# Two-block transformer kernel: 512-column pairing of the two activation halves in the residual and up stages, with a reduce and an in-place product on VectorE

## The reference, cut to what matters

```python
x = x + mixed @ w_out[l]                      # layers 0 and 1: 1024 x 1024
h = rms_norm(x, norm_ffn[l])
up = h @ w_up[l]                              # 1024 x 5632
a, bval = up[..., :D_FF], up[..., D_FF:]      # D_FF = 2816
a = conv(a, conv_w, width 3) + conv_b
x = x + (silu(a) * bval) @ w_down[l]          # 2816 x 1024
...
x = x + mix @ w_out                           # layer 2 (the second block)
m = rmsnorm(x, norm_mlp_w)
u = relu(m @ w_ff1)                           # 1024 x 4096
x = x + (u * u) @ w_ff2                       # 4096 x 1024
```

## Time and profile before

| | us |
|---|---|
| median of three runs | 1192.5 |
| lowest and highest run | 1192.38, 1197.29 |
| span of the profiled execution, first to last instruction | 1191.5 |
| TensorE busy (matmuls) | 1145.0 |
| VectorE busy | 725.3 |
| ScalarE busy | 586.5 |
| GpSimd busy | 358.4 |
| mean granted TensorE clock, share of full | 0.981 |

### The profile page before, as it was taken

The page is one execution under the profiler, slowest core; times in us unless marked ns, Lnnn a source line. Parts: engine busy times, 40 slices in busy tenths (PEclk is TensorE's granted clock), DMA queues, the critical chain, the costliest instruction groups (busy, mean ns, idle before and its releaser), DMA issues.

```text
span 1191.5 us, 21228 instructions
## 1 busy us (share of the span) xinstructions
PE 1145.0 (96%) x9016; PEld 1107.0 (93%) x9016; DVE 725.3 (61%) x1077; ACT 586.5 (49%) x800; POOL 358.4 (30%) x215
## 2 busy tenths in 40 slices
PE   6999999999999999999899999999889989999997
PEld 5998989999999999899899999998789989999996
DVE  5742227777576665222777766767778657756663
ACT  5444337555354635443755544566554646443432
POOL 3025644322022212645432302323443125101021
PEclk8999999999999999999999999998889989999999
DMA  8634334454754664343355475454322135573741
GB/s 282 204 106 142 107 116 150 160 177 137 252 178 130 194 209 141 106 135 114 110 174 177 157 232 178 147 166 146 93 71 72 54 124 184 162 219 123 238 133 58
DMA packets 172766, 180.43 MB, mean 151 GB/s; under 512 B 4224, under 2 KB 170496, under 8 KB 172544
## 3 DMA queue, kind: packets, MB, share of 16 engines
q1 hardware_dynamic: 172672, 179.08, 46.6%
HBM read 178.02 MB, written 1.05 MB: 150 GB/s over the span
## 4 chain that ended last, share of the span: by engine, by line
PE 72%; issue 11%; DVE 9%; ACT 5%; POOL 2%; DMA 1%; SPq 0%; POOLq 0%; DVEq 0%; ACTq 0%
PE psum L569 71%; ACT sb_w_hi L1064 2%; DVE sb_scratch L1498 2%; DVE sb_w_lo L1507 1%; POOL sb_scratch L2200 1%; PE psum L726 1%; DVE sb_rs L1546 1%; DVE sb_rs L1498 1%; ACT sb_scratch L1064 1%; DMA sb_raw<-in_w_in 1%; ACT sb_rs L1064 1%; DVE sb_xt L1498 0%; DVE sb_scratch L1927 0%; PE psum L800 0%; DVE sb_scratch L1747 0%
## 5 line engine op out<-in xcount | busy, mean ns | idle before, releaser
L569 PE MATMUL psum<-sb_xg_hi,sb_w_hi 128*128 128x256 f32 x1664 | 485.3, 292 | 4.5 <-DVE sb_w_lo L1507 3.1
L569 PE MATMUL psum<-sb_xg_lo,sb_w_hi 128*128 128x256 f32 x1664 | 474.6, 285 | 0.0
L569 PE MATMUL psum<-sb_xg_hi,sb_w_lo 128*128 128x256 f32 x1664 | 474.2, 285 | 0.0
L1507 DVE TENSOR_TENSOR sb_w_lo<-sb_raw,sb_w_hi 128x2048 fp32r<-128x2048 f32 (+3 forms) x147 | 301.2, 2052 | 129.1 <-ACT sb_w_hi L1064 129.1
L1064 ACT ACTIVATE sb_w_hi<-sb_raw 128x2048 fp32r<-128x2048 f32 (+3 forms) x189 | 319.6, 1698 | 118.2 <-PE psum L569 65.2
L569 PEld LDWEIGHTS psum<-sb_xg_hi,sb_w_hi 128*128 128x128 f32 x1664 | 323.1, 194 | 14.6 <-issue 10.3
L569 PEld LDWEIGHTS psum<-sb_xg_lo,sb_w_hi 128*128 128x128 f32 x1664 | 323.3, 194 | 0.7
L569 PEld LDWEIGHTS psum<-sb_xg_hi,sb_w_lo 128*128 128x128 f32 x1664 | 323.0, 194 | 0.0
L569 PE MATMUL psum<-sb_hid_hi,sb_w_hi 128*128 128x256 f32 x864 | 247.5, 286 | 8.8 <-DVE sb_hid_lo L1572 8.0
L2155 POOL TENSOR_TENSOR sb_w_lo<-sb_raw,sb_w_hi 128x2048 fp32r<-128x2048 f32 (+1 forms) x42 | 188.1, 4478 | 212.6 <-ACT sb_w_hi L1064 212.6
L569 PE MATMUL psum<-sb_hid_lo,sb_w_hi 128*128 128x256 f32 x864 | 245.5, 284 | 0.0
(11 more groups left out here) (144 smaller groups left out, 1006.1 us busy)
## 6 DMA issues: line engine op xcount, KB each, us to landing
sb_raw<-in_w_in SPq DMA_DIRECT2D x52, 1024.0 KB, 5.1
sb_raw<-in_w_up SPq DMA_DIRECT2D x44, 1024.0 KB, 5.1
sb_raw<-in_w_ff SPq DMA_DIRECT2D x16, 1024.0 KB, 5.5
sb_raw<-in_w_down SPq DMA_DIRECT2D x16, 768.0 KB, 4.4
sb_raw<-in_w_down SPq DMA_DIRECT2D x16, 640.0 KB, 4.1
sb_raw<-in_w_ff SPq DMA_DIRECT2D x16, 640.0 KB, 4.0
sb_raw<-in_w_out SPq DMA_DIRECT2D x8, 1024.0 KB, 5.0
sb_raw<-in_w_ff SPq DMA_DIRECT2D x8, 768.0 KB, 4.4
```

The costliest lines, as they stand in the source:

```text
L569: return nc.tensor.matmul(ps, lhsT, rhs, start=start, stop=stop, skip_group_check=True)
L1507: v.tensor_tensor(part(w_lo, s), part(raw, s), part(w_hi, s).bitcast(F32), ALU.subtract)\
```

## The change

For tiles of the kinds x, fa, fb and f2 a chunk's first two matmuls, which have the same weights (`hi`), become one of 512 columns: its moving operand is the chunk's high and low activation side by side, for which `xg_hi`/`xg_lo` and `hid_hi`/`hid_lo` become halves of one buffer. The left half of the bank gathers high by high and low by high, the right half high by low. Such a tile fills a bank of its own, and `Plan.place` deals the banks out; other kinds still share a bank in twos. The reader sums the halves. An x tile is added in two steps, left half and then right half, with a wait of VectorE for itself between them. In fa, fb and f2 tiles `tensor_reduce` sums both halves of the bank into SBUF in one pass, VectorE waits for that, and the product of before follows in place, reading SBUF only. The bank's reader is now the reduce (`a_sum`, `h_sum`, `r_sum`). `paired` gives the last tile of a bank, so a wide tile's reader waits for that tile alone.

```diff
@@ READERS, class Plan @@
+               "pb": ["yb_gated"], "x": ["x_tile"], "fa": ["a_sum"], "fb": ["h_sum"], "conv": ["c_tile"],
+               "ba": ["ba_tile"], "lg": ["lg_tile"], "z": ["z_tile"], "f2": ["r_sum"]}
+    WIDE = ("x", "fa", "fb", "f2")
+    def place(self):
+        self.banks, self.at = [], []
+        for t, kind in enumerate(self.kinds):
+            if kind in self.WIDE or t % 2 == 0:
+                self.banks.append([])
+            self.at.append((len(self.banks) - 1, len(self.banks[-1])))
+            self.banks[-1].append(t)
@@ build @@
-        xg_hi = sb("xg_hi", KD * T, F32R)
-        xg_lo = sb("xg_lo", KD * T, F32R)
+        xg_both = sb("xg_both", 2 * KD * T, F32R)
+        xg_hi, xg_lo = xg_both[:, 0:KD * T], xg_both[:, KD * T:]
...
         def main_bank(t):
-            return psum[:, t // 2 % RING, t % 2 * T:(t % 2 + 1) * T]
+            n, half = plan.at[t]
+            return psum[:, n % RING, half * T:(half + 1) * T]
+        def wide_bank(t):
+            return psum[:, plan.at[t][0] % RING, :].rearrange("p (two c) -> p two c", two=2)
         def paired(t):
-            return t // 2 * 2 + 2
+            return plan.banks[plan.at[t][0]][-1] + 1
@@ main_tile @@
-                if first and t % 2 == 0 and t >= 2 * RING:
-                    for name, value in plan.readers[t - 2 * RING] + plan.readers[t - 2 * RING + 1]:
-                        if q.due(name, value):
-                            pe.wait_ge(S[name], value)
+                bank, half = plan.at[t]
+                if first and half == 0 and bank >= RING:
+                    for before in plan.banks[bank - RING]:
+                        for name, value in plan.readers[before]:
+                            if q.due(name, value):
+                                pe.wait_ge(S[name], value)
...
+                    ends = last and k == s.chunks - 1
+                    if plan.kinds[t] in plan.WIDE:
+                        i = act[3] + k0 + k
+                        pair = split_pair(act[4])[:, :, i * T:(i + 1) * T]
+                        mul(wide_bank(t), hi[:, k, c], pair, first and k == 0, False)
+                        mm = mul(main_bank(t), lo[:, k, c], pair[:, 0, :], False, ends)
+                        continue
@@ x_add @@
-                v.tensor_tensor(tl(xt, m), tl(xt, m), main_bank(t), ALU.add).then_inc(S["x_tile"], 1)
+                parts = wide_bank(t)
+                v.tensor_tensor(tl(xt, m), tl(xt, m), parts[:, 0, :], ALU.add).then_inc(S["dve_step"], q.one("dve_step"))
+                dve.wait_ge(S["dve_step"], q.sent["dve_step"])
+                v.tensor_tensor(tl(xt, m), tl(xt, m), parts[:, 1, :], ALU.add).then_inc(S["x_tile"], 1)
+            def sum_wide(out_, t, signal):
+                v.tensor_reduce(out_, wide_bank(t).rearrange("p two c -> p c two"), mybir.AxisListType.X, ALU.add)\
+                    .then_inc(S[signal], q.one(signal))
+                dve.wait_ge(S[signal], q.sent[signal])
@@ up slabs of layers 0 and 1 @@
-                            ps = main_bank(t)
                             if s.kind == "fa":
-                                v.tensor_tensor(tl(AB, r, T + 2)[:, 2:], ps, RSTD, ALU.mult).then_inc(S["a_tile"], 1)
+                                a = tl(AB, r, T + 2)[:, 2:]
+                                sum_wide(a, t, "a_sum")
+                                v.tensor_tensor(a, a, RSTD, ALU.mult).then_inc(S["a_tile"], 1)
                             else:
+                                sum_wide(tl(h32, r), t, "h_sum")
                                 dve.wait_ge(S["a_scaled"], q.next("a_scaled"))
-                                v.tensor_tensor(tl(h32, r), ps, tl(s_scaled, r), ALU.mult).then_inc(S["h_tile"], 1)
+                                v.tensor_tensor(tl(h32, r), tl(h32, r), tl(s_scaled, r), ALU.mult).then_inc(S["h_tile"], 1)
@@ up slabs of layer 2 @@
-                        stt(tl(y_conv, i % 4), main_bank(t), 0.0, RSTD, ALU.max, ALU.mult)\
+                        r = tl(y_conv, i % 4)
+                        sum_wide(r, t, "r_sum")
+                        stt(r, r, 0.0, RSTD, ALU.max, ALU.mult)\
                             .then_inc(S["r_tile"], 1)
```

More of the change, by code:

```diff
@@ L208, in __init__ @@
         self.readers = []
+        self.kinds = []
         self.counts = {}
@@ L252, in __init__ @@
             self.down((2, "down", half), w["w_ff2_2"][0], f0, n)
+        self.place()
         lows = {"split_lo": 0, "pool_lo": 0}
@@ L284 @@
     READERS = {"s": ["s_tile"], "rope": ["q_raw", "q_cos"], "v": ["v_tile"], "gate": ["gate_raw"], "pa": ["ya_gated"],
-               "pb": ["yb_gated"], "x": ["x_tile"], "fa": ["a_tile"], "fb": ["h_tile"], "conv": ["c_tile"],
-               "ba": ["ba_tile"], "lg": ["lg_tile"], "z": ["z_tile"], "f2": ["r_tile"]}
+               "pb": ["yb_gated"], "x": ["x_tile"], "fa": ["a_sum"], "fb": ["h_sum"], "conv": ["c_tile"],
[8 more added lines that the diff above has]
+            self.banks[-1].append(t)
     def tile(self, slab, kind):
         slab.tiles.append(len(self.readers))
+        self.kinds.append(kind)
         pairs = []
@@ L339 @@
     "gate_raw", "gate", "ya_gated", "yb_gated", "mixed",
-    "a_tile", "a_tap", "a_conv", "a_silu", "a_scaled", "h_tile", "r_tile", "r_square",
+    "a_sum", "h_sum", "r_sum", "a_tile", "a_tap", "a_conv", "a_silu", "a_scaled", "h_tile", "r_tile", "r_square",
     "c_tile", "c_tap", "c_conv", "c_silu", "ba_tile", "lg_tile", "z_tile", "z_silu",
@@ L369, in build @@
         xt = sb("xt", KD * T)
-        xg_hi = sb("xg_hi", KD * T, F32R)
-        xg_lo = sb("xg_lo", KD * T, F32R)
-        hid_hi = sb("hid_hi", HID * T, F32R)
-        hid_lo = sb("hid_lo", HID * T, F32R)
+        xg_both = sb("xg_both", 2 * KD * T, F32R)
+        xg_hi, xg_lo = xg_both[:, 0:KD * T], xg_both[:, KD * T:]
+        hid_both = sb("hid_both", 2 * HID * T, F32R)
+        hid_hi, hid_lo = hid_both[:, 0:HID * T], hid_both[:, HID * T:]
         cst = sb("consts", CONSTS.shape[1])
@@ L456, in main_bank, with split_pair @@
         def main_bank(t):
-            return psum[:, t // 2 % RING, t % 2 * T:(t % 2 + 1) * T]
+            n, half = plan.at[t]
+            return psum[:, n % RING, half * T:(half + 1) * T]
+        def wide_bank(t):
+            return psum[:, plan.at[t][0] % RING, :].rearrange("p (two c) -> p two c", two=2)
         def paired(t):
-            return t // 2 * 2 + 2
+            return plan.banks[plan.at[t][0]][-1] + 1
+        def split_pair(both):
+            return both.rearrange("p (two c) -> p two c", two=2)
         def by_chunk(buf, s):
@@ L594, in main_tile @@
                     for i, (a, b) in enumerate(trio):
-                        mm = mul(ps, a, b, first and k == 0 and i == 0 and t % 2 == 0, last and k == s.chunks - 1 and i == 2)
+                        mm = mul(ps, a, b, first and k == 0 and i == 0 and half == 0, ends and i == 2)
                 if last:
@@ L633, in token_factor @@
                 mm.then_inc(S["rtok_sum"], 1)
-            xg = (xg_hi, xg_lo, "xg_lo")
-            hid = (hid_hi, hid_lo, "hid_lo")
+            xg = (xg_hi, xg_lo, "xg_lo", 0, xg_both)
+            hid = (hid_hi, hid_lo, "hid_lo", 0, hid_both)
             xg_base = hid_base = 0
@@ L1032, in between @@
                         spread_out()
-                slab_two(s, (hid_hi[:, GH * T:], hid_lo[:, GH * T:], "hid_lo"), hid_base, between)
+                slab_two(s, (hid_hi[:, GH * T:], hid_lo[:, GH * T:], "hid_lo", GH, hid_both), hid_base, between)
             hid_base += LT
```

## The result

The changed kernel takes 1236.5 us (median of 4 runs, 1233.3 to 1239.7), the kernel before 1193.2 us beside it: ratio 1.036, 95% interval 1.034 to 1.038. It is slower, as forecast, and inside the range, but by 3.6% where the forecast had 2.1%. The profiled execution has a span of 1231.5 us, 40.0 us longer than the one before; it is the fastest of the four runs (1233.3 us), so stages are compared with spans and not with the median.

A forecast was written before the change was run, and what follows sets the result against it. The prediction took the ring of ScalarE, VectorE and GpSimd to bound layers 0 and 1's first up stages, TensorE most other stages. Layers 0 and 1 +31.9, layer 2 and end -6.6: +25.3 on 1192.5, 1218 us; range 1198 to 1250.

The forecast's parts named there:

- the ring: Up stages, layers 0 and 1: ScalarE, VectorE and GpSimd wait on each other; 11.94 us a slab pair becomes 14.34.
- cheap reduce: Rival: the reduce takes only 0.42 us, so the kernel gets faster, 1176 us; chance 0.05.
- slow reduce: Rival: the reduce takes 1.19 us, and VectorE also bounds layer 2's up stages, 1258 us; chance 0.13.
- GpSimd doesn't block: Rival: in up stages GpSimd's scaling doesn't hold VectorE's SBUF product; ring +1.79 us, total 1204 us; chance 0.12.
- wide matmuls give nothing: Rival: a chunk keeps its 0.36 us, so pairing gains nothing on TensorE, 1237 us; chance 0.13.
- The clock: Rival: TensorE's idle time in the ring halves its clock, 1 us more in each of 22 pairs, 1240 us; chance 0.05.
- VectorE's ring sets the end there: First up stages, layers 0 and 1: TensorE's idling until the first reduce costs nothing while VectorE's ring is slower.
- a chunk 24 ns less: Wide tiles on TensorE: a 512-column and a 256-column matmul take 0.336 us a chunk instead of 0.36.
- The first down stages: Layers 0 and 1, after the first up stage: 80 chunks counted as gaining, -1.9 us each.
- layer 2's first up stage: Nine tiles remain after the first reader, ending 24.95 us behind it against 23.7 before: +1.25 us.
- The ring of banks: Wide tiles fill a bank: three tiles, not three pairs, precede the first reader; free in layers 0 and 1, +1.25 us in layer 2.
- the last down stages: Layers 0 and 1, after the second up stage: 67 chunks counted as gaining, -1.6 us each.

The follow-up runs named there:

- The first experiment: The changed kernel with fa and fb tiles of layers 0 and 1 narrow again (pairing only in residual stages and layer 2): 1191.4 us, ratio 0.998.
- the control: The kernel before the change, with ScalarE's weight split moved ahead of its taps and copies in the up stages of layers 0 and 1: 1189.3 us, ratio 0.996.

## Why the prediction was right in sign and short in size

**Right: the ring.** Counted from the `fb` split, the forecast had the sums at 2.21 and 3.30, ScalarE's split at 5.01, the last product's end at 12.04; the trace has 2.20, 3.27, 4.95 and 11.78. The sum's price was 0.68 and is 0.682; the product was to be held by GpSimd and took 0.87 (shown by the sum in another bank, 0.42). Ring 14.08 for 14.34, and the up stages +13.25 and +7.05 for +13.9 and +6.5. The rivals "cheap reduce", "slow reduce" and "GpSimd doesn't block" fall on these rows, and "wide matmuls give nothing" on 0.347 to 0.353 us a chunk. "The clock" falls for the ring: its gaps of 1.0 and 1.4 us twice a pair leave 1.00, and the half clock comes only behind the stalls at the starts of first up stages. In layers 0 and 1 the forecast's reason that VectorE's ring sets the end there covers it; it was not tested by itself.

The span came out 14.7 us longer than the sum. By stage, 18.6 us of misses upward stand against 3.9 downward (the first up stages of layers 0 and 1, layer 2's in and out), so a part of the error cancelled by luck.

**Short: the term "a chunk 24 ns less".** This is the largest mis-sized term. I took 0.216 for the wide matmul from the plain fp32 statistics, and left the narrow one at 0.120; the rows show 0.23 to 0.24 and 0.115 to 0.12. A chunk saves 13 ns in layer 2, and 7 to 13 in layers 0 and 1, not 24. Layer 2's 416 chunks make 416 x 0.0107 = 4.5 us of the 14.7, the 390 of layers 0 and 1 between 4.2 and 6.7. Layer 2's stages show it bare: 27.74 for 28.80. The first down stages, -0.45 and -0.5 for -1.9, are this term: at 0.353 a chunk their 80 counted chunks give 1.4 us less each. Neither layout nor order changes it.

**Short: layer 2's first up stage, +4.56 for +1.25.** The ring of banks was counted, but two things not. The norm's first reader comes 13.4 us after the stage's start (12.5 before), by all that is known for the adds before it (with the adds alone left of the change the stage is 0.9 longer than before); and from that reader to the end it takes 27.4 us, not the forecast's 24.95: behind the stall the matmuls run at half clock for 3.4 us, from 1050.5 to 1053.9, which costs 1.7, and 72 chunks cost 0.8 more. Together with the 0.9 that is 3.4, for 3.3 missing. With the stall shortened by early sums the stage is 37.4.

**Short: the last down stages, +0.75 and +2.2 for -1.6.** I let the ring's delay end with the up stage. The first experiment, without the ring, has them at 28.27 and 28.59 us, so 1.3 and 2.5 us are the ring's backlog on VectorE, and more if one reckons from the 27.74 that 80 chunks can take; how the backlog spreads over its splits and adds was not taken apart.

**Not seen: how much slack lay one instruction away.** The forecast described the ring with ScalarE's split "in line behind" the taps and took it as fixed. The added 2.1 us a pair cost some 40 us because VectorE's work and ScalarE's split stood in series; side by side, the whole change costs some 4 us beside the kernel before and 8 beside the control with the same order.

## What to carry to other kernels

Fewer and wider matmuls save little where their columns stay the same, here 7 to 13 of 360 ns, and the sums that they push onto an engine in a dependency ring lengthen it (four sums of 0.68 us, a ring 2.14 us longer): before widening, compare that engine's own work per turn with TensorE's, and apply the change by stage. When an engine's turn grows, look first at what waits in program order behind it on the next engine; moving that one instruction was worth more than every edit to the sums. Gains that draw on the same idle time don't add, so price each edit again on the kernel that has the others. And compare stages that have the same code before crediting an edit with 3 us in 1200.

## What the runs showed of the hardware

- An fp32r matmul of 512 columns is followed by the next after 0.230 to 0.241 us, one of 256 columns behind it after 0.114 to 0.120, one of 256 in a train of its kind after 0.120, all at the full granted clock. Contiguous or split columns, alternating or two by two make no difference beyond 0.15 us in 80 chunks.
- A pair of the two takes 0.3467 us in long trains, and in others of the same code a mean of 0.3533 (27.73 and 28.27 us for 80 pairs); what chooses is not known.
- The Trainium skill (TensorE: Matmul & The Clock Gate, Back-to-back issue gap) gives N/2.4 + 2.5 ns for a single matmul, an estimate of 216 and 109 ns; the trace shows more in every case, and the trace decides.
- A sum of two halves of a bank by a reduce costs what 512 elements cost (682 ns), although it writes 256; into PSUM 691 ns.
- VectorE's split with two SBUF inputs and GpSimd's two scalings (1.82 us with no split beside them): when the split starts first it keeps 2.29 us and the scalings take 3.22; when the first scaling starts 0.3 us ahead, the split takes 2.83 and the scalings 3.72.
- TensorE's granted clock fell to 0.50 for 3.4 us behind idle times of 2.99 and 2.85 us in the changed kernel, and stayed at 1.00 behind one of 2.87 in the first experiment and through the ring's gaps of 1.0 and 1.4 us.
